# Index tables of a mixture-of-experts block: marks laid out densely, first gather and odd shared products moved

## The reference

```python
def reference(x, ...):
    xn  = rms_norm(x, norm1_g)
    z   = xn @ w_in
    mix = concat(rms_norm(spatial_gating(gelu(z[:, :1024]))), rms_norm(fourier_mix(z[:, 1024:])))
    h   = x + mix @ w_out
    hn  = rms_norm(h, norm2_g)                       # 1024 tokens x 1024
    eidx, gates = route(hn, w_router, router_bias)   # top 8 of 64 experts for each token
    routed = sum over a token's 8 experts of gate * ((silu(hn @ w_gate[e]) * (hn @ w_up[e])) @ w_down[e])
    shared = (silu(hn @ ws_gate) * (hn @ ws_up)) @ ws_down
    return rms_norm(h + routed + shared, final_norm_g)
```

## Time and profile before

| | before |
|---|---|
| median of 3 runs | 1337.76 us (1336.47 to 1339.56) |
| the profiled execution's own time | 1338.38 us |
| its span | 1336.7 us |
| TensorE busy | 1294.2 us, 97% |
| weight loads of TensorE | 1046.9 us, 78% |
| VectorE busy | 858.6 us, 64% |
| ScalarE busy | 773.7 us, 58% |
| GpSimd busy | 468.3 us, 35% |

### The profile page before, as it was taken

One profiled execution on the slowest core, in us unless ns is written; L12 is line 12 of the kernel. 1 busy time (PEld: TensorE's weight loads), 2 busy tenths in 40 slices (PEclk: granted clock), 3 DMA queues, 4 the chain that ended last, 5 costly groups with the idle time before them and its releaser, 6 DMA issues.

```text
span 1336.7 us, 26923 instructions
## 1 busy us (share of the span) xinstructions
PE 1294.2 (97%) x6095; PEld 1046.9 (78%) x6096; DVE 858.6 (64%) x1226; ACT 773.7 (58%) x1077; POOL 468.3 (35%) x604
## 2 busy tenths in 40 slices
PE   6999988999998999999999999999999999999996
PEld 5885466888776788888888888888888888888885
DVE  5430444458833677767776777767776777767767
ACT  5320234223243677777776777677776777677763
POOL 2431301001002444444444444444444444444464
PEclk9999988999997999999999999999999999999999
DMA  9204032212146799999999999999999999999989
GB/s 343 91 1 157 0 126 95 95 64 95 41 157 213 264 328 339 319 311 321 329 332 329 321 322 342 323 326 328 348 318 330 320 347 330 312 318 325 346 234 265
DMA packets 81268, 337.65 MB, mean 253 GB/s; under 512 B 12624, under 2 KB 15696, under 8 KB 64592
## 3 DMA queue, kind: packets, MB, share of 16 engines
q1 hardware_dynamic: 53872, 251.19, 48.7%
q0 software_dynamic: 27360, 86.01, 26.5%
HBM read 288.59 MB, written 65.27 MB: 265 GB/s over the span
## 4 chain that ended last, share of the span: by engine, by line
PE 91%; DMA 2%; DVE 2%; ACT 1%; issue 1%; POOL 1%; POOLq 0%; ACTq 0%; SPq 0%; DVEq 0%
PE ps L833 37%; PE ps_out L847 18%; PE ps L504 7%; PE ps L663 7%; PE ps L521 7%; PE ps L557 4%; PE ps L698 3%; PE ps L855 1%; PE ps_out L724 1%; PE ps L731 1%; PE ps L605 1%; DMA yb_in<-y_rows_dram 1%; PE ps_out L680 1%; DMA Xg<-hn_rows_dram,idxg 1%; DVE ya_in L1724 1%
## 5 line engine op out<-in xcount | busy, mean ns | idle before, releaser
L833 PE MATMUL ps<-w_gu,xTh 128*128 x1488 | 467.6, 395 | 1.0 <-DVE xTl L1647 1.0
L1446 DVE TENSOR_TENSOR w_gu<-raw_gu,w_gu (+1 forms) x256 | 296.5, 1219 | 78.3 <-ACT w_gu L1129 78.3
L833 PEld LDWEIGHTS ps<-w_gu,xTh 128*128 128x128 f32 x1488 | 273.4, 188 | 54.4 <-issue 1.5
L833 PE MATMUL ps<-w_gu,xTl 128*128 x744 | 291.0, 391 | 0.0
L1129 ACT ACTIVATE w_gu<-raw_gu (+1 forms) x256 | 250.0, 1048 | 0.1
L847 PE MATMUL ps_out<-w_dn,hTh 128*128 x744 | 242.2, 407 | 0.0
L1858 POOL DMA_INDIRECT y_rows_dram<-ob,idxs x90 | 147.1, 1635 | 141.9 <-ACT ob L1152 134.8
L1453 DVE TENSOR_TENSOR w_dn<-raw_dn,w_dn (+1 forms) x128 | 151.2, 1223 | 26.1 <-ACT w_dn L1133 23.5
L833 PEld LDWEIGHTS ps<-w_gu,xTl 128*128 128x128 f32 x744 | 139.6, 188 | 28.8
L847 PEld LDWEIGHTS ps_out<-w_dn,hTh 128*128 128x128 f32 x744 | 133.1, 189 | 25.4 <-issue 0.2
L847 PE MATMUL ps_out<-w_dn,hTl 128*128 x372 | 145.9, 392 | 0.0
(11 more groups left out here) (277 smaller groups left out, 1689.4 us busy)
## 6 DMA issues: line engine op xcount, KB each, us to landing
raw_gu<-in_w_gate SPq DMA_DIRECT2D x64, 1024.0 KB, 7.7
raw_gu<-in_w_up SPq DMA_DIRECT2D x64, 1024.0 KB, 11.8
raw_dn<-in_w_down SPq DMA_DIRECT2D x64, 1024.0 KB, 12.7
x_ring<-in_x SPq DMA_DIRECT2D x8, 512.0 KB, 4.7
w_in_sb<-in_w_in SPq DMA_DIRECT2D x8, 512.0 KB, 10.1
xh<-in_x SPq DMA_DIRECT2D x8, 512.0 KB, 7.4
w_out_sb<-in_w_out SPq DMA_DIRECT2D x1, 4096.0 KB, 12.9
hn_rows_dram<-rows SPq DMA_DIRECT2D x8, 512.0 KB, 2.6
```

What stands on the lines that cost most here:

```text
L833: mm = pe.matmul(ps[3][:, :], x_[:, k, :], w_gu[:, bass.ds(at, 1), part, :, k, :], start=(k == 0 and part == 0 and x_ is xTh), stop=(k == ...
L1446: dv.tensor_tensor(gu_part(w_gu[:, :, 1, :, :, :], at, m), gu_part(raw_gu, at, m), gu_part(w_gu[:, :, 0, :, :, :], at, m).bitcast(F32), AL ...
```

## The change

1. `mark` and `pick` change their layout: the pick's number k stands ahead of the item or the place, so that the matmul's operands `pick[:, c, k, :]` and `mark[:, c, k, :]` are dense.
2. VectorE writes its comparison to a buffer of its own, `new_mark`, in the old layout (item, then k). ScalarE reads it in that order and writes the product to `mark` through a rearranged view: successive elements go 272 bytes apart. VectorE's comparison of the places now runs over `count_row` (136 numbers) with `place8` repeated along the inner dimension.
3. `new_mark` is one buffer for all pairs, so `two_marks(pair)` waits until ScalarE is done with the pair before; ScalarE in turn waits with pairs 2 and 3 for the tables of two pairs earlier.
4. Odd `shared_down` products go into banks 0 and 4, the even ones stay in `ps_out`. A `shared_down` now waits for the `shared_out` two chunks back, and `shared_down(1)` for `s_tab`. An odd `shared_out` is two ScalarE instructions of 512 columns.
5. Item 0's rows are gathered to `Xg_first`, a place of their own, and that gather stands ahead of GpSimd's wait for `s_q`. `Xg_first` and `mark` lie where w_dn's second half will be, so ScalarE waits for the first gate copy (`s_gt`) ahead of `split_dn(1)`.
6. TensorE's order: tables 0 stays behind gu(5); then down 2, gu(6) first half, turn 5, tables 1, gu(6) second half, down 3, tables 2, gu(7) whole with turn 6 inside, tables 3, down 4, turn 7, down 5, down 6, the rows of item 0, down 7, gate_up(0). Item 0 has no down product any more. ScalarE does shared_out 6 ahead of evac_xT(0) and shared_out 7 behind it, ahead of `split_dn(1)`.

```diff
-        pick = [place("pick0", [P, 2, P, TOPK], F16, R_AT), ...]
+        pick = [place("pick0", [P, 2, TOPK, P], F16, R_AT), ...]
-        mark = place("mark", [P, 4, TAB, TOPK], F16, W_AT + 2176)
+        new_mark = place("new_mark", [P, 2, TAB, TOPK], F16, W_AT + 2176)
+        Xg_first = place("Xg_first", [P, GATED], F32, W_AT + 16 * KB)
+        mark = place("mark", [P, 4, TOPK, TAB], F16, W_AT + 16 * KB + GATED * 4)
...
                 if c == 0:
...
+                elif c == 1:
+                    pe.wait_ge(s_tab, 1)
                 else:
-                    pe.wait_ge(s_y0, c)
+                    pe.wait_ge(s_y0, c - 1)
...
-                            mm = pe.matmul(ps[6 + half][:, :], h_[:, k, :], w_[:, k, cols_],
+                            mm = pe.matmul(ps[((6, 7), (0, 4))[c % 2][half]][:, :], h_[:, k, :], w_[:, k, cols_],
...
-                    mm = pe.matmul(ps[5][:, 0:TAB], pick[c // 2 % 2][:, c % 2, :, k], mark[:, c % 4, :, k],
+                    mm = pe.matmul(ps[5][:, 0:TAB], pick[c // 2 % 2][:, c % 2, k, :], mark[:, c % 4, k, :],
...
             two_tables(0)
             shared_down(2)
-            two_tables(1)
             shared_gu(6, (0, 1))
             shared_turn(5)
+            two_tables(1)
             shared_gu(6, (2, 3))
+            shared_down(3)
             two_tables(2)
-            shared_down(3)
             shared_gu(7, (0, 1))
             shared_turn(6)
+            shared_gu(7, (2, 3))
             two_tables(3)
-            shared_gu(7, (2, 3))
             shared_down(4)
             shared_turn(7)
             shared_down(5)
+            shared_down(6)
...
-                if isinstance(i, int) and i == 0:
-                    shared_down(NC - 1)
...
             turn_item(0, 1)
-            shared_down(6)
+            shared_down(NC - 1)
             gate_up(0, *expert(0))
...
             def marks_by_token(pair):
                 act.wait_ge(s_pick, pair + 1)
-                for c in (2 * pair, 2 * pair + 1):
-                    m = mark[:, c % 4, :, :].rearrange("p j k -> p (j k)")
-                    ins = act.activation(m, m, ACT.Copy, scale=token[:, c:c + 1])
+                if pair >= 2:
+                    act.wait_ge(s_table, 2 * (pair - 1))
+                at = pair % 2 * 2
+                for r in range(2):
+                    c = 2 * pair + r
+                    ins = act.activation(mark[:, at + r, :, :].rearrange("p k j -> p j k"), new_mark[:, r, :, :], ACT.Copy,
+                                         scale=token[:, c:c + 1])
...
             def two_marks(pair):
+                if pair >= 1:
+                    dv.wait_ge(s_mtok, pair)
                 if pair >= 2:
                     dv.wait_ge(s_table, 2 * (pair - 1))
...
                       dv.tensor_tensor(pick[pair % 2][:, :, :, :],
-                                       count8[:, None, 1:P + 1, :].to_broadcast([P, 2, P, TOPK]),
-                                       place8[:, both, None, :].to_broadcast([P, 2, P, TOPK]), ALU.is_equal)))
+                                       count_row[:, None, None, 1:P + 1].to_broadcast([P, 2, TOPK, P]),
+                                       place8[:, both, :, None].to_broadcast([P, 2, TOPK, P]), ALU.is_equal)))
...
-            gp.wait_ge(s_q, NC)
             gp.wait_ge(s_idx, 2)
             gp.wait_ge(s_dz, 32)
-            for i in range(TURN):
+            gather(0, 0)
+            gp.wait_ge(s_q, NC)
+            for i in range(1, TURN):
                 gather(i, i)
```

More of the change, by code:

```diff
@@ L138, in build @@
         gb_row = place("gb_row", [P, DA], F32, R_AT + 10 * KB)
[L139 removed]
+        pick = [place("pick0", [P, 2, TOPK, P], F16, R_AT), place("pick1", [P, 2, TOPK, P], F16, R_AT + 6 * KB + 256)]
         rt_a = place("rt_a", [P, NC, NE], F32, R_AT + 4 * KB)
         count8 = place("count8", [P, TAB, TOPK], F16, W_AT)
[L142 to L144 removed]
+        new_mark = place("new_mark", [P, 2, TAB, TOPK], F16, W_AT + 2176)
+        hs2 = place("hs2", [P, 2, F], F32, W_AT + 10624)
+        hh2 = place("hh2", [P, 2, F], F32, W_AT + 10624 + 2 * KB)
+        Xg_first = place("Xg_first", [P, GATED], F32, W_AT + 16 * KB)
+        mark = place("mark", [P, 4, TOPK, TAB], F16, W_AT + 16 * KB + GATED * 4)
         count_row = place("count_row", [P, TAB], F16, R_AT + 10 * KB + 768)
@@ L817, in _ @@
             shared_down(5)
+            shared_down(6)
             def turn_item(u, fills):
                 pe.wait_ge(s_ga[u], 16 * fills)
-                turn_rows(Xg[:, u, :], (1, 2)).then_inc(s_tr, 1)
+                turn_rows(Xg_first[:, :] if u == 0 and isinstance(fills, int) and fills == 1 else Xg[:, u, :], (1, 2)).then_inc(s_tr, 1)
             def gate_up(i, e, at):
@@ L1115, in shared_out @@
                     act.wait_ge(s_shst[c % 2], 16 * (c // 2))
-                act.activation(ob[:, c % 2, :], ps_out[:, :], ACT.Copy).then_inc(s_y0, 1)
+                if c % 2 == 0:
+                    act.activation(ob[:, 0, :], ps_out[:, :], ACT.Copy).then_inc(s_y0, 1)
+                else:
+                    act.activation(ob[:, 1, 0:512], ps[0][:, :], ACT.Copy)
+                    act.activation(ob[:, 1, 512:D], ps[4][:, :], ACT.Copy).then_inc(s_y0, 1)
             def marks_by_token(pair):
                 act.wait_ge(s_pick, pair + 1)
-                for c in (2 * pair, 2 * pair + 1):
-                    m = mark[:, c % 4, :, :].rearrange("p j k -> p (j k)")
-                    ins = act.activation(m, m, ACT.Copy, scale=token[:, c:c + 1])
+                if pair >= 2:
[5 more added lines that the diff above has]
+                                         scale=token[:, c:c + 1])
                 ins.then_inc(s_mtok, 1)
@@ L1174, in item @@
                 evac_xT(i + 1)
-                if isinstance(i, int) and i == 0:
-                    shared_out(NC - 1)
-                else:
+                if not (isinstance(i, int) and i == 0):
                     now = now or expert(i)
@@ L1236, in _ @@
             shared_out(5)
+            shared_out(6)
             act.wait_ge(s_tab, 1)
@@ L1239, in _ @@
             evac_xT(0)
-            shared_out(6)
+            shared_out(NC - 1)
             act.wait_ge(s_rd, 1)
+            act.wait_ge(s_gt, 1)
             split_dn(1)
@@ L1604, in two_marks @@
                 both = slice(2 * pair, 2 * pair + 2)
-                at = pair % 2 * 2
-                many((dv.tensor_tensor(mark[:, at:at + 2, :, :], count8[:, None, :, :].to_broadcast([P, 2, TAB, TOPK]),
+                many((dv.tensor_tensor(new_mark[:, :, :, :], count8[:, None, :, :].to_broadcast([P, 2, TAB, TOPK]),
                                        item8[:, both, None, :].to_broadcast([P, 2, TAB, TOPK]), ALU.is_equal),
                       dv.tensor_tensor(pick[pair % 2][:, :, :, :],
-                                       count8[:, None, 1:P + 1, :].to_broadcast([P, 2, P, TOPK]),
-                                       place8[:, both, None, :].to_broadcast([P, 2, P, TOPK]), ALU.is_equal)))
+                                       count_row[:, None, None, 1:P + 1].to_broadcast([P, 2, TOPK, P]),
+                                       place8[:, both, :, None].to_broadcast([P, 2, TOPK, P]), ALU.is_equal)))
                 dv.sem_inc(s_pick, 1)
@@ L1831, in gather @@
                 gp.sem_inc(s_turn, 1)
-                gp.indirect_dma_start(out=Xg[:, u, :], out_offset=None, in_=hn_d[:, :],
+                gp.indirect_dma_start(out=Xg_first[:, :] if isinstance(i, int) and i == 0 else Xg[:, u, :], out_offset=None, in_=hn_d[:, :],
                                       in_offset=bass.IndirectOffsetOnAxis(ap=idxg[:, u:u + 1], axis=0),
@@ L1841, in keep_gate @@
                 gp.sem_inc(s_turn, 1)
-                gp.tensor_copy(gate[:, u:u + 1], Xg[:, u, bass.ds(e + D, 1)]).then_inc(s_gt, 1)
+                from_ = Xg_first if isinstance(i, int) and i == 0 else Xg[:, u, :]
+                gp.tensor_copy(gate[:, u:u + 1], from_[:, bass.ds(e + D, 1)]).then_inc(s_gt, 1)
                 gp.wait_ge(s_gt, i + 1)
```

## The result

The changed kernel takes 1347.68 us in the median of 4 runs (1347.18 to 1348.09); the kernel before, beside it on the same chip, 1337.31 us (1336.47 to 1339.56). The ratio is 1.0072 (95% interval 1.0057 to 1.0087): some 10 us slower, where 10.5 us faster was forecast. It lies outside the range. All ratios here leave out one disturbed execution of the kernel before, of 2549.66 us, in a later group; they are estimated from all other runs and can differ from the quotient of two medians by up to 0.0008.

A forecast was written before the change was run, and what follows sets the result against it. TensorE was taken as the bound, so an earlier loop start comes out whole: gate_up(2) 13.4 us earlier, minus 0.5 schedule error and 2.4 clock, gives 10.5 off 1337.8: 1327.3 us, range 1320 to 1334.

The forecast's parts named there:

- What ScalarE pays: ScalarE's mark instruction, writing each number 272 bytes from the last: 2.3 us instead of 1.19, 4.6 a pair.
- The bound of 3.6: Upper limit in us for one ScalarE mark instruction: L1020's whole 2.2 ns an element on top of 1.19.
- the rival of the other side: ScalarE's stepped writes alone decide; beyond 3.6 us a mark instruction the kernel is slower, at 4.2 it takes 1342; chance 0.08.
- The rest of the sum: VectorE-ScalarE round trip: from 363.9, four comparisons of 3.6, four mark pairs of 4.6, plus 2.0 and 0.3, giving 399.0 us.
- the edge of 3.3: ScalarE's stepped mark write: ns an element, 3.6 us an instruction, beyond which the kernel would be slower than before.
- Tables, 1.4 us a pair: TensorE's table matmuls with dense operands: 1.4 us a pair instead of 4.0, between 1.0 and 1.8, 10.4 us less work.
- tables still 4 us: Rival: TensorE's tables stay at 4 us a pair, the step not their cause; 6.7 us later, 1333; chance 0.05.
- VectorE, 2.3 us for the picks: VectorE's comparison of picks, one operand repeating an element along the inner dimension: 2.3 us, between 1.2 and 2.35.
- The wait ahead of turn 5: TensorE waits 4.3 us there for VectorE's shared_h(5), queued behind comparison 2.
- The clock: TensorE falls to the lower level behind turn 5's wait, costing it 2.3 us, some 2 of it reaching tables 3.
- From the tables to the loop: Indices at 402.0, first gather at 403.5 taking 8 us (6 to 9.4), gate_up(0) until 420.7, gate_up(2) at 433.1.
- `Xg_first` and the banks at nothing: GpSimd's first gather gains little from its own place; the bank waits cost nothing, and down 5's 1 us wait goes.

The follow-up runs named there:

- experiment 1: The kernel before with 36 added ScalarE copies, nine forms four times each on idle buffers; the changed kernel's form took 4.97 us, and the program's time says nothing.
- Experiment 5: The changed kernel with ScalarE reading `new_mark` at a step of 16 bytes and writing `mark` densely; 1324.64 us, ratio 0.9903 to the kernel before.
- experiment 2: The changed kernel with VectorE comparing marks straight into the new layout, ScalarE multiplying densely in place, no `new_mark`; 1321.18 us, ratio 0.9883 to the kernel before.
- experiment 3: The changed kernel with the old table layouts, comparisons and in-place multiplication; only order, banks and first gather stay changed; 1328.37 us, ratio 0.993 to the kernel before.
- experiment 11: The kernel of experiment 10 with tables 3 ahead of shared_gu(7)'s second half; 1322.13 us, ratio 0.9885 to the kernel before.
- experiments 8 and 9: Each the kernel of experiment 2: 8 without `Xg_first`, first gather behind `s_q`, 1319.47 us; 9 with all shared down products in `ps_out`, 1318.8 us.
- experiment 10: The kernel of experiment 2 with shared_h(5) ahead of the third pair's comparisons on VectorE; 1320.25 us, ratio 0.9869 to the kernel before.

## Why the prediction was wrong

**The step that failed is a term of the sum: "What ScalarE pays".** The mechanism stood there, and was even named as the one that decides; the size was wrong. 2.3 us was taken for a mark instruction, with 3.6 as the upper bound; it takes 5.0, and the sum has eight of them one behind the other. The error is in the choice of the row. L1020 writes float32 words, and it is exact for them (1116 ns by itself, experiment 1). The mark is a halfword, and a halfword written at such a step costs 4.6 to 4.8 ns, over twice a word's 2.0 to 2.2. The bound of 3.6 was only this row once more, its whole rate put on top of the dense duration, and so no bound for another size of element. The case that came true was the rival of the other side, at 0.08 ("beyond 3.6 us an instruction ... slower; at 4.2, 1342").

The Trainium skill (Vector Engine (DVE) Microarchitecture Reference, 5.2) gave an estimate of 1.9 to 2.8 us by its price of a hopping write, which is for 4-byte words on VectorE. The measurement of halfwords on ScalarE, 4.97 us, is nearly twice the upper end; that price does not carry over.

**The rest of the sum, with 5.0 put in.** Eight mark instructions in the round trip: 363.9 + 14.4 + 8 x 5.0 + 2.3 = 420.6 us for the end of marks 3; it was 419.75. The added 8 x 2.7 = 21.6 us are within 1.2 us of what the total missed: 1347.7 - 1327.3 = 20.4. Experiment 5 tests the same from the other end: with a mark instruction at 2.24 us, near the 2.3 of the forecast, the kernel takes 1324.6 us, against 1327.3 forecast; two terms of the clock are off there and cancel (see there). The sum also has two slips: it puts some 2 us to the clock and takes off 2.4, and L1020 lies 1.1 ns an element below the edge of 3.3, not 1.1 us. Neither changes the outcome.

**Tables, 1.4 us a pair**: they took 1.0, the lower bound, where the clock was full (0.98 in experiment 2), and 2.0 at the lower level. In the same order of TensorE the old layout costs 4.0 us a pair (experiment 3) and the dense one 0.98 (experiment 2), so the step of the operands was their cause; which of the two operands it is was not tried. The rival "tables still 4 us" is out.

**VectorE, 2.3 us for the picks**: 2.28. The rule of the Trainium skill (the same page, 5.1), a repeated element runs at one a cycle where a step of one ran at two, agrees with this row: 2.28 us, and 1.21 before.

**The wait ahead of turn 5**: 9.5 us instead of 4.3, in the place and by the releaser forecast; 3.9 in experiment 5.

**The clock**: the lower level behind that wait was as forecast. With the waits of 4.3 and 6.2 us for the tables there were two stretches more, and a fourth in gate_up(1). Until tables 3 the round trip, not TensorE, set the time, so the first two stand nowhere on the chain. The last two lie on the chain of waits: tables 3 took 2.0 us instead of 1.0, down 4 4.65 instead of 2.75, gate_up(1) 7.36 instead of 5.7 (experiment 2). How much of these 4.6 us reached the end no run shows, since a store sets the pace in between.

**From the tables to the loop**: the gather took 5.0 us here and 8.1 to 8.3 in experiments 2 and 5 (8 taken, bounds 6 to 9.4). In the changed kernel the chain does not run through it, but through the store of chunk 4 that shared_out(6) waits for. The change moves shared_out 6 ahead of evac_xT(0), and the prediction didn't ask what that step is itself waiting for (here a store of 4.85 us); experiment 11 met this again. `Xg_first` and the banks at nothing: right, as far as experiments 8 and 9 show it, in the kernel of experiment 2.

**The signs of the parts.** Order, banks and first gather take off 8.5 us, dense tables could take off 11 by themselves and 16 together with them; the rearranged write costs some 26 against the dense comparison (1347.7 against 1321.2).

## What to carry to other kernels

Where an unknown access pattern decides, the nearest row must agree in the size of the element as well as in engine and step; if it doesn't, what it gives is no bound, and the chance of the other side is larger than it looks. If a layout has to be turned, put the step on the reading side, or let VectorE compare straight into the new layout. For a pair of chunks ScalarE then has 4.5 us (experiment 5), or 2.4 us and VectorE 1.1 more than before (experiment 2), against 10.0 here. And when a step is moved ahead of another on an engine's queue, look up what the moved one waits for, transfers included.

## What the hardware showed unexpectedly

- ScalarE, 128 partitions, time per element written, overhead of the instruction included (experiment 1; one execution, four instructions of each form): float16 dense 1.02 ns, 4 bytes apart 1.30, 16 bytes apart 4.81, 32 bytes 4.56, 272 bytes 4.57; float32 32 bytes apart 2.18, 544 bytes apart 1.97. Reading float16 16 bytes apart and writing densely 1.94.
- TensorE, float16, 128 x 128 by 128 x 136: 250 ns each with both operands at a step of 16 bytes, some 60 ns densely.
- Taking away a wait of 1 us (experiment 10) brought gate_up(0) 0.9 us forward, but gate_up(1) then took 7.34 us at a granted clock of 0.77, where it took 5.74 us at 1.00 in experiment 2, behind a wait of the same length.
- The same transfer differs much from kernel to kernel: the gather of item 0's rows took 5.0 us in the changed kernel and 8.1 in experiment 2, the store of chunk 4 took 4.85 us in the changed kernel and 9.8 in experiment 11. What beside them makes the difference was not tried.
